# A hybrid decoder layer on one core: the transposed half of a triangular inverse made by transposing, and decode's value products moved to GpSimd

## The chip, the cores and the metric

The program runs on one core of one Trainium2 chip. Its time is the device time of one execution in microseconds; before the change the median of 3 runs was 1231.72 us (1231.1 to 1231.84). The profile shows one further execution.

## What is computed

One layer of a hybrid decoder is applied to a prompt of 512 tokens and to a sample group of 8 sequences with one token each. RMSNorm is followed by one input projection (2048 to 8208 columns), in which two mixers have their parts. All of it is fp32.

- Mixer A: softmax attention of 8 heads of 128 under three windows, (128,1), (512,4) and (2048,16), with RoPE on 32 dimensions. For a sample token, the keys and values of its 2048 cached positions are gathered: 128 keys for each of the three windows, and the token's own key in each of them. `o = softmax(q k^T / sqrt(128)) v`, merged over the windows by denominators, which is one softmax over 384 + 3 x 1 keys.
- Mixer B: gated DeltaNet, 8 heads of 128: causal convolution of width 4 and SiLU on q, k, v, then a delta rule in chunks. It needs the inverse of a triangular matrix:

```
a_mat = where(strict, einsum('bhnid,bhnjd->bhnij', kbeta, kc) * decay, 0.0)
t_mat = triangular_solve(a_mat + eye, eye, left_side=True, lower=True)
u = t_mat @ (v * beta);   w = t_mat @ (kbeta * exp(gcum))
```

- Both outputs are gated by SiLU of their own columns, go through one output projection, a norm and the residual.

## The kernel before

**Projection.** A weight tile (128 columns, 16 blocks of 128 rows) is split into a high and a low part in fp32r: ScalarE rounds `w_raw` to `w_hi` (`hi`, line 1006), and `w_lo` is the difference, made by VectorE for quarters 0 and 2 (`lo`, 1384) and by GpSimd for quarters 1 and 3 (`lo`, 1966). The hidden state is split the same way. TensorE's `segment` (583) does a quarter of a tile for one half of the tokens. Segments of half 0 have 8 wide and narrow matmuls, those of half 1 have 12. The half 0 result stands in one PSUM bank as two sums, which VectorE's `half_out` (1409) adds and copies out in segment 4 of a tile; the next tile's half 0 waits for that (`proj_half`).

**Steps.** A head has 8 tiles, 8 segments each: 64 steps, numbered 0 to 63. On every engine the same loop `stretch` runs: in each step it takes each of a list of generators one `yield` further, in the list's order, and after that the engine's own part of the projection is done (on VectorE `half_out` in segment 4, then `lo` in segments 0 and 4; on GpSimd `lo` in segments 2 and 6; on ScalarE `hi` in even segments; on SyncE the load of a weight quarter in even segments). `idle(n)` is n empty steps. So the order of each engine's instructions is written out by hand, and semaphores make an engine wait where another is behind. Work of head h-1's attention (`tail_a`, `attn_decode`) runs in head h's 64 steps, and after head 7 in a tail of 40 steps beside the output projection.

**Mixer B in the steps** (`mix_b`, lines 750, 1196, 1606, 2000; `own_b` makes the convolutions, `mix_q` q's part). A = kk^T times decay is made for four chunks of 128 tokens at once as a symmetrised matrix. The inverse is built by doubling the block size in levels n = 1 to 6. Two copies are kept: `b_U` holds the inverse of one orientation and `b_T` its transpose (chunks 0, 1 of U are one orientation and chunks 2, 3 the other, and the reverse in T). At each level: Y = B x T (line 801) into PSUM; ScalarE copies Y to `b_Y`; Z_U = Y^T x U (812) and Z_T = U^T x Y (820), blockwise; VectorE subtracts Z_U from U and Z_T from T (1658, 1659), and the next level begins. A level takes two steps; level 1 begins in step 36. B for each level is the masked A, made by GpSimd (2015).

**Decode of mixer A** (`attn_decode`, lines 430, 893, 1263, 1800). Scores are transposed (900), soft-maxed by 8 rows (1266 and 1803 to 1816), the probabilities transposed back with keys on partitions (906), and copied to `pT`. The values lie as keys x (sequence, dimension), one 128x1024 tile for each window, in `V_TILE`. ScalarE scales each 128x128 block by its column of pT (1281, 24 instructions), VectorE adds the three tiles (1819, 1822), and TensorE sums over the keys with eight products with a column of ones (911).

**RoPE** of q and k (`own_a`, 1515) is three instructions of VectorE on 32 rows (1511 to 1513).

Of the kernel before, what the change touches and what calls it, by code (L numbers as in the profile page):

```python
# [70 lines left out]
def layout(x):  # L71
# [8 lines left out]
    for name, order in (("cache_win_k", (0, 1, 2)), ("cache_win_v", V_ORDER)):  # L80
        c = x[name][0]
        windows = [c[:, PAST - 128:PAST], c[:, PAST - 512:PAST:4], c[:, 0:PAST:16]]
        t[name] = np.stack([windows[n] for n in order]).transpose(3, 0, 2, 1, 4)
# [91 lines left out]
def build(nc, x_prompt, x_sample, cache_k, cache_v, state_conv, state_delta, g_pre, w_in, w_ba, conv_w, a_log, dt_bias,  # L175
          onorm_w, w_out, g_post, c_ident, c_upper, c_causal, c_levels, c_lnmask, c_rope, c_terms,
          y_p, y_s, k_new, v_new, c_new, c_old, st_p, st_s):
    scratch_q = nc.dram_tensor("scratch_q", (NH, NB, HD), F32, kind="Internal").ap()
    scratch_g = nc.dram_tensor("scratch_g", (KT, P, TP), F32, kind="Internal").ap()

    with ExitStack() as ctx:
# [100 lines left out]
        pT = sb("pT", [P, 4, NB])  # L282
# [11 lines left out]
        xs_res = (S0[0:NB].rearrange("p b e -> p (b e)"), qb[0:NB])  # L294
        K_TILE, V_TILE = (kv[:, 0], kv[:, 1], kv[:, 0]), (kv[:, 1], kv[:, 0], qb[:])
# [25 lines left out]

        def mx(n):
            return MX[:, n].rearrange("p (c d) -> p c d", c=NC)
# [17 lines left out]
            "mix_kk mix_qk mix_A mix_QK mix_B mix_U0 mix_T_ps mix_T mix_Y_ps mix_Y mix_Z mix_UT ch_kS ch_r "  # L341
            "ch_v_ps ch_v ch_S_ps ch_o_ps ch_S ch_o1 ch_o o_sq on_rs o_n o_T z_sig_b z_ok_b gated_b gB_out S_out "

            "qkp qb_in kb0_in kb1_in kb2_in prod red sc_T sc_max p_exp p_norm p_T pT_ok vb0_in "
            "vb1_in vb2_in pv_sum pv_ps gated_ad "
# [22 lines left out]
        def _(sp):  # L368
# [61 lines left out]
            def attn_decode(hh, at=10):  # L430
# [3 lines left out]
                for n in (1, 2):  # L434
                    sp.dma_start(V_TILE[n].rearrange("p (b d) -> p b d", b=NB), cache_v[hh, V_SLOT[n]]).then_inc(
                        s[f"vb{n}_in"], 16)

            def attn_rows(h):
# [14 lines left out]
                if not first:  # L453
                    sp.wait_ge(s["pv_ps"], h)
# [54 lines left out]
            def early_rows():  # L509
                yield from idle(30)  # L510
                sp.wait_ge(s["gB_out"], 16 * (NH - 1))
                sp.wait_ge(s["gA_out"], 16 * (NH - 1))
                for k in (4, 5, 9):
                    load_row(k)
                yield from idle(25)
# [22 lines left out]
            work = [late_rows(), attn_decode(h, 6)]  # L538
# [43 lines left out]
        def _(pe):  # L582
# [167 lines left out]
            def mix_b(h):  # L750
# [3 lines left out]
                yield from idle(24)  # L754
                pe.wait_ge(s["kv_silu"], 2 * h + 2)
# [7 lines left out]
                for c in chunks:  # L763
                    last = pe.transpose(mx(1)[:, c, :], xv[:, c * P:(c + 1) * P], ident[:])
                last.then_inc(s["mix_T1"], 1)
# [4 lines left out]
                yield from idle(3)  # L770
# [20 lines left out]
                yield from idle(2)  # L791
                for n in range(1, LEVELS):
# [13 lines left out]
                    if n == 1:  # L806
                        pe.wait_ge(s["mix_U0"], 3 * h + 3)
                        pe.wait_ge(s["mix_ss"], 2 * NC * h + 2 * NC)
                        pe.wait_ge(s["mix_QK"], h + 1)
                    if n < LEVELS - 1:  # L810
                        for j in range(2):
                            last = pe.matmul(crossed(mx(2), n, True, j), b_Y[:, j, :], crossed(b_U, n, True, j),  # L812
                                             start=True, stop=True)
                    else:
# [7 lines left out]
                    last.then_inc(s["mix_Z"], 1)  # L822
# [28 lines left out]
            def mix_q(h):  # L851
                yield from idle(35)
                pe.wait_ge(s["q_silu"], h + 1)
                pe.wait_ge(s["mix_kbT"], h + 1)
                for c in range(NC):
                    last = pe.transpose(mx(2)[:, c, :], cq[:, c * P:(c + 1) * P], ident[:])
                last.then_inc(s["mix_T1"], 1)
                pe.wait_ge(s["mix_arg"], h + 1)
                for c in range(NC):
                    last = pe.matmul(mx(3)[:, c, :], xk[:, c * P:(c + 1) * P], cq[:, c * P:(c + 1) * P], start=True,  # L860
# [32 lines left out]
            def attn_decode(hh, late=0, sums=12, norm=5):  # L893
                yield from idle(17 + late)
# [7 lines left out]
                yield from idle(norm)  # L902
# [1201 lines left out]
```

## Time and profile before

| | |
|---|---|
| timed runs, median of 3 | 1231.72 us |
| the profiled execution | 1230.87 us |
| its span, first to last instruction | 1229.0 us |
| TensorE (PE) busy | 1201.0 us, 98% |
| weight loads (PEld) busy | 1123.0 us, 91% |
| VectorE (DVE) busy | 793.9 us, 65% |
| ScalarE (ACT) busy | 518.4 us, 42% |
| GpSimd (POOL) busy | 303.5 us, 25% |
| mean granted TensorE clock | 0.996 |
| moved by DMA | 151.55 MB, mean 123 GB/s |

The span is the time from the first to the last instruction; the profiled execution's own time holds 1.9 us more. Busy times overlap between engines. Matmuls are pipelined, so the record of one (0.28 us) is longer than the distance to the next (0.12 us); what a piece of work takes from TensorE is read from starts, not from durations. An fp32 matmul leaves two records, a transpose or an fp32r matmul one.

### The profile page before, as it was taken

The page shows a single profiled execution, that of the slowest core. Times are in us where ns is not written, and L with a number is a line of the kernel's source. Part 1 is how long each engine was busy: PE and PEld are TensorE (multiplying, and loading weights), DVE is VectorE, ACT ScalarE, POOL GpSimd, SP SyncE. Part 2 cuts the span into 40 slices and gives each one's busy share as a digit, 9 for nine tenths or more (in the row PEclk, how much of TensorE's full clock was granted, in tenths as well). Part 3 has the DMA queues.
Part 4 walks back from the last instruction along what each step waited for, and adds up shares of the span by engine and source line. Part 5 has one row for each costly group of instructions (what it writes and reads, how often), then busy time and mean ns, then how long its engine had stood idle before and what let it go on. Part 6 is the DMA issues. An engine that isn't in the chain of part 4 may idle for free.

```text
span 1229.0 us, 25525 instructions
## 1 busy us (share of the span) xinstructions
PE 1201.0 (98%) x8793; PEld 1123.0 (91%) x8793; DVE 793.9 (65%) x1945; ACT 518.4 (42%) x1376; POOL 303.5 (25%) x275
## 2 busy tenths in 40 slices
PE   5999999999999999999999999999999999999997
PEld 4899999999999999999999999999999998999996
DVE  5576577657765776577657765676567658365544
ACT  6443334533453345334533453345334536532211
POOL 0114121412141224122412241124212322322211
PEclk8999999999999999999999999999999999999999
DMA  7332453245324531453245324432453266232253
GB/s 244 100 95 63 141 165 104 63 140 166 103 63 141 164 103 63 143 163 103 63 144 162 104 62 144 161 104 62 147 159 104 88 196 202 82 103 78 93 207 139
DMA packets 79645, 151.55 MB, mean 123 GB/s; under 512 B 12353, under 2 KB 22242, under 8 KB 77986
## 3 DMA queue, kind: packets, MB, share of 16 engines
q1 hardware_dynamic: 78254, 148.78, 38.9%
q10 hardware_dynamic: 1312, 1.59, 0.5%
q8 instruction: 64, 1.05, 0.3%
q14 instruction: 15, 0.12, 0.0%
HBM read 132.20 MB, written 17.27 MB: 122 GB/s over the span
## 4 chain that ended last, share of the span: by engine, by line
PE 82%; DVE 8%; ACT 4%; issue 3%; DMA 1%; SPq 0%; DVEq 0%; ACTq 0%
PE PJ L614 17%; PE PJ L610 11%; PE PJ L611 10%; PE PJ L612 10%; PE PJ L615 9%; PE MX L820 3%; PE MX L801 2%; DVE memx L1578 1%; PE PJ L933 1%; PE MX L812 1%; PE MX L744 1%; PE MX L724 1%; PE PJ L934 1%; PE PJ L935 1%; PE MD L872 1%
## 5 line engine op out<-in xcount | busy, mean ns | idle before, releaser
L1966 POOL TENSOR_TENSOR w_lo<-w_raw,w_hi 128x512 fp32r<-128x512 f32 x160 | 218.1, 1363 | 808.2 <-ACT w_hi L1006 808.2
L614 PE MATMUL PJ<-h,w_hi 128*128 128x512 f32 x1110 | 416.8, 412 | 0.0
L610 PE MATMUL PJ<-h,w_hi 128*128 128x264 f32 (+1 forms) x1216 | 354.8, 292 | 0.0
L611 PE MATMUL PJ<-h,w_hi 128*128 128x264 f32 (+1 forms) x1216 | 344.7, 284 | 0.0
L612 PE MATMUL PJ<-h,w_lo 128*128 128x264 f32 (+1 forms) x1216 | 344.6, 283 | 0.0
L615 PE MATMUL PJ<-h,w_lo 128*128 128x256 f32 x1110 | 310.7, 280 | 0.0
L614 PEld LDWEIGHTS PJ<-h,w_hi 128*128 128x128 f32 x1110 | 208.9, 188 | 43.3 <-DVE w_lo L1384 1.7
L1006 ACT ACTIVATE w_hi<-w_raw 128x512 fp32r<-128x512 f32 x320 | 196.6, 624 | 91.3 <-PE PJ L612 79.1
L611 PEld LDWEIGHTS PJ<-h,w_hi 128*128 128x128 f32 x1216 | 229.6, 189 | 2.3
L610 PEld LDWEIGHTS PJ<-h,w_hi 128*128 128x128 f32 x1216 | 229.4, 189 | 0.0
L612 PEld LDWEIGHTS PJ<-h,w_lo 128*128 128x128 f32 x1216 | 228.2, 188 | 0.0
L615 PEld LDWEIGHTS PJ<-h,w_lo 128*128 128x128 f32 x1110 | 209.4, 189 | 2.8 <-issue 1.7
L1384 DVE TENSOR_TENSOR w_lo<-w_raw,w_hi 128x512 fp32r<-128x512 f32 x160 | 120.1, 756 | 131.5 <-ACT w_hi L1006 125.9
L1022 ACT ACTIVATE memx<-memx 128x520 f32<-128x520 f32 x32 | 20.2, 633 | 107.0 <-DVE memx L1589 107.0
L1578 DVE SCALAR_TENSOR_TENSOR memx<-memx,cw 128x512 f32<-128x512 f32 x72 | 61.2, 850 | 1.7
L1788 DVE CUSTOM_DVE_ANT_0 kv<-kv,qb 128x128 f32<-128x128 f32 x192 | 54.9, 342 | 2.5 <-DMA qb<-scratch_q 2.5
L1223 ACT ACTIVATE mem<-MX 128x256 f32<-128x256 f32 x48 | 18.3, 381 | 87.9 <-PE MX L801 87.9
L1658 DVE TENSOR_TENSOR mem<-mem,MX 128x256 f32<-128x256 f32 (+1 forms) x48 | 19.1, 398 | 54.5 <-PE MX L820 54.5
L933 PE MATMUL PJ<-h,w_hi 128*128 128x256 f32 (+1 forms) x160 | 47.3, 296 | 1.0 <-DVE h L1845 1.0
L2015 POOL TENSOR_TENSOR mem<-mem,levels 128x256 f32<-128x256 f32 x48 | 39.2, 817 | 26.6 <-PE MX L801 15.7
L1415 DVE TENSOR_REDUCE memx<-PJ 128x256 f32<-128x512 f32 x63 | 43.0, 683 | 3.6 <-DVE memx L1589 1.6
L934 PE MATMUL PJ<-h,w_hi 128*128 128x256 f32 (+1 forms) x160 | 45.1, 282 | 0.0
(334 smaller groups left out, 1841.2 us busy)
## 6 DMA issues: line engine op xcount, KB each, us to landing
w_raw<-in_w_in SPq DMA_DIRECT2D x256, 256.0 KB, 2.7
w_raw<-in_w_out SPq DMA_DIRECT2D x64, 256.0 KB, 2.9
kv<-in_cache_win_k SPq DMA_DIRECT2D x24, 512.0 KB, 4.6
kv<-in_cache_win_v SPq DMA_DIRECT2D x16, 512.0 KB, 4.9
out<-memx SPq DMA_DIRECT2D x16, 260.0 KB, 3.8
mem<-in_x_prompt SPq DMA_DIRECT2D x4, 1024.0 KB, 10.0
S<-in_state_delta SPq DMA_DIRECT2D x8, 512.0 KB, 3.4
out<-S SPq DMA_DIRECT2D x8, 512.0 KB, 2.9
```

Of the source, the lines that this page charges most:

```text
L610: pe.matmul(ps, wh, h_hi[:, k, tok], start=k == 0, stop=False)
L611: pe.matmul(ps, wh, h_lo[:, k, tok], start=False, stop=False)
L612: last = pe.matmul(ps, wl, h_hi[:, k, tok], start=False, stop=end)
L614: pe.matmul(both, wh, h2[:, :, k, tok], start=k == 0, stop=False)
L615: last = pe.matmul(ps, wl, h_hi[:, k, tok], start=False, stop=False)
L933: pe.matmul(out, wh, h_hi[:, k, tok], start=start and i == 0, stop=False)
L934: pe.matmul(out, wh, h_lo[:, k, tok], start=False, stop=False)
L1006: act.activation(w_hi[:, par, 4 * q:4 * q + 4, :], w_raw[:, q, :, :], ACT.Copy).then_inc(s["w_hi_ok"], 1)
L1384: dve.tensor_tensor(w_lo[:, par, 4 * q:4 * q + 4, :], w_raw[:, q, :, :], w_hi[:, par, 4 * q:4 * q + 4, :].bitcast(F32), ALU.subtract).then ...
L1578: link(dve.scalar_tensor_tensor(acc[:, 0:TP], xq[:, i:i + TP], w[:, 24 + i:25 + i], acc[:, 0:TP], ALU.mult, ALU.add))
L1788: last = dve.tensor_tensor_reduce(out=x, in0=x, in1=qb[:, b * HD:(b + 1) * HD], scale=1.0, scalar=0.0, op0=ALU.mult, op1=ALU.add, accum_ou ...
L1966: pool.tensor_tensor(w_lo[:, par, 4 * q:4 * q + 4, :], w_raw[:, q, :, :], w_hi[:, par, 4 * q:4 * q + 4, :].bitcast(F32), ALU.subtract).the ...
```

## The change

Two edits are made together.

**Inverse.** Level n = 1 to 5 no longer computes Z_T by products. Z_U goes to PSUM in an order in which the pair of orientations stands side by side (`merged` in place of `crossed`), ScalarE copies it to `b_Y[:, 2:4]`, VectorE subtracts it from U there, and one step later TensorE transposes the two 128x128 blocks into MX bank 3, from which VectorE subtracts T's update. A level takes three steps instead of two, and level 1 begins in step 34. TensorE:

```
 if n < LEVELS - 1:
     for j in range(2):
-        last = pe.matmul(crossed(mx(2), n, True, j), b_Y[:, j, :], crossed(b_U, n, True, j), start=True, stop=True)
+        last = pe.matmul(merged(mx(2), n, True, j), b_Y[:, j, :], crossed(b_U, n, True, j), start=True, stop=True)
+    last.then_inc(s["mix_Z"], 1)
+    yield
+    pe.wait_ge(s["mix_Zs"], (LEVELS - 2) * h + n)
+    for j in range(2):
+        last = pe.transpose(mx(3)[:, j, :], b_Y[:, 2 + j, :], ident[:])
+    last.then_inc(s["mix_Z"], 1)
...
-    last.then_inc(s["mix_Z"], 1)
-    for c in chunks if n < LEVELS - 1 else (2, 3):
-        last = pe.matmul(blocks(mx(3)[:, c, :], n, c // 2), b_U[:, c, :],
-                         blocks(b_Y[:, c % 2, :], n, c // 2), start=True, stop=True)
```

ScalarE and VectorE:

```
+                    if n < LEVELS - 1:
+                        act.wait_ge(s["mix_Z"], UTS * h + 2 * n - 1)
+                        act.activation(b_Y[:, 2:4, :], mx(2)[:, 0:2, :], ACT.Copy).then_inc(s["mix_Zs"], 1)
+                        yield
...
-                        u, uz = crossed(b_U, n, True), crossed(mx(2), n, True)
-                        t, tz = crossed(b_T, n, False), crossed(mx(3), n, False)
+                        u, uz = crossed(b_U, n, True), merged(b_Y[:, 2:4, :], n, True)
+                        t, tz = crossed(b_T, n, False), merged(mx(3), n, False)
...
                     dve.tensor_tensor(u, u, uz, ALU.subtract).then_inc(s["mix_UT"], 1)
+                    if n < LEVELS - 1:
+                        yield
+                    dve.wait_ge(s["mix_Z"], UTS * h + 2 * n)
                     dve.tensor_tensor(t, t, tz, ALU.subtract).then_inc(s["mix_UT"], 1)
```

**Steps that move with it.** `mix_b` begins a step earlier on every engine (TensorE 24 to 23, ScalarE 24 to 23, VectorE 25 to 24, GpSimd 22 to 21). v's transposes go a step behind k's. The convolution of q in VectorE's `own_b` begins in step 27 instead of 28 (`idle((10, 2, 6)[j])` becomes `(10, 2, 5)`), RoPE of q in step 44 instead of 43, k's stays in step 51. `mix_q` uses MX bank 0 in place of banks 2 and 3, and its products come two steps behind its transposes (37 instead of 35), behind ScalarE's squares; b_QK is made in VectorE's step 37 instead of 36.

**Decode's values.** The host lays the values out as dimension x (sequence, key). The normalised probabilities (8 x 384) are written to DRAM and read back three times, each to all 128 partitions, into `P_TILE` (the place of `probs` and `probT`). GpSimd multiplies the three 128x1024 tiles, VectorE adds them and reduces over the keys; ScalarE's 24 scalings, pT, the three small transposes and the eight one-column products are gone. The decode begins four steps earlier (TensorE 17 to 13). GpSimd and SyncE:

```
+            def attn_decode(hh, at=23):
+                yield from idle(at)
+                for n in range(3):
+                    if n == 0:
+                        pool.wait_ge(s["vb0_in"], 16 * hh + 16)
+                        pool.wait_ge(s["pb_in"], 48 * hh + 48)
+                    elif n == 1:
+                        pool.wait_ge(s["vb_in"], 32 * hh + 32)
+                    pool.tensor_tensor(V_TILE[n], V_TILE[n], P_TILE[n], ALU.mult).then_inc(s["prod"], 1)
+                    yield
+                    yield
...
+                yield from idle(out)
+                sp.wait_ge(s["p_norm"], hh + 1)
+                sp.dma_start(scratch_p[hh].rearrange("n b t -> b n t"), pd).then_inc(s["p_out"], 16)
+                yield from idle(back)
+                sp.wait_ge(s["p_out"], 16 * hh + 16)
+                sp.wait_ge(s["attn_ps"], hh + 1)
+                for n in range(3):
+                    sp.dma_start(P_TILE[n], scratch_p[hh, n].rearrange("b t -> (b t)").partition_broadcast(P)).then_inc(
+                        s["pb_in"], 16)
+                    yield
```

with out=7 and back=2: the store in SyncE's step 17, the broadcasts in 19, 20 and 21. VectorE:

```
-            def attn_decode(hh, late=0, sums=(9, 1, 4)):
-                yield from idle(17 + late)
+            def attn_decode(hh, late=0, gap=31):
+                yield from idle(13 + late)
...
-                yield from idle(sums[0])
+                yield from idle(gap)
                 dve.wait_ge(s["prod"], 3 * hh + 2)
                 link(dve.tensor_tensor(V_TILE[0], V_TILE[0], V_TILE[1], ALU.add))
-                yield from idle(sums[1])
+                yield
                 dve.wait_ge(s["prod"], 3 * hh + 3)
                 dve.tensor_tensor(V_TILE[0], V_TILE[0], V_TILE[2], ALU.add).then_inc(s["pv_sum"], 1)
-                yield from idle(sums[2])
+                yield
+                dve.wait_ge(s["pv_sum"], hh + 1)
+                dve.tensor_reduce(pv[:], V_TILE[0].rearrange("p (b t) -> p b t", b=NB), AX.X, ALU.add).then_inc(
+                    s["pv_ok"], 1)
+                yield
```

The sums are in steps 47 and 48 instead of 42 and 46. In the tail after head 7, the products are in GpSimd's steps 22, 24 and 26 and the sums, the reduction and the gate in VectorE's 27 to 30. The loads of three gated rows into places that `P_TILE` shares wait for head 6's products.

## Rows read from the trace of the kernel before

**Rows 1.** Table by windows, one whole head; busy us of each engine, then clock, DMA.
```profile
core 0: us, PE busy (x) PEld busy (x) DVE busy (x) ACT busy (x) POOL busy (x), PEclk, DMA share, GB/s
526.00:648.70 122.70, 122.49 (x894) 114.32 (x893) 82.83 (x213) 54.28 (x152) 31.33 (x29) 1.00 0.39 119
```

**Rows 2.** Waits of TensorE: waiting line, releaser, us in total, times, longest.
```profile
PE MX L856 <- DVE memx L1698: 1.5, 7, 0.2
```

**Rows 3.** Instructions in order of time, one level of the inverse: start, duration, what.
```profile
593.57 0.61 PE L812 MATMUL MX<-mem 128*128 128x128 f32 x4
594.02 1.00 PE L820 MATMUL MX<-mem 128*128 128x64 f32 x8
594.83 0.37 PE L610 MATMUL PJ<-h,w_hi 128*128 128x264 f32 x1
595.03 0.28 PE L611 MATMUL PJ<-h,w_hi 128*128 128x264 f32 x1
...
596.36 0.60 PE L801 MATMUL MX<-mem 128*128 128x128 f32 x4
596.72 0.37 PE L610 MATMUL PJ<-h,w_hi 128*128 128x264 f32 x1
...
597.00 0.39 ACT L1223 ACTIVATE mem<-MX 128x256 f32<-128x256 f32 x1 [2.01 <-PE MX L801]
```

**Rows 4.** The same view, two transposes of A between two segments.
```profile
580.39 0.38 PE L784 MATMUL MX<-ident,mem 128*128 128x128 f32 x2
580.53 0.48 PE L614 MATMUL PJ<-h,w_hi 128*128 128x512 f32 x1
```

**Rows 5.** The same view, decode's one-column products and small transposes.
```profile
567.41 0.33 PE L906 MATMUL MD<-ident,rb 8*128 8x8 f32 x3
567.67 0.66 PE L761 MATMUL MX<-ident,memx 128*128 128x128 f32 x4
...
620.01 1.84 PE L911 MATMUL MD<-ones,kv 128*128 128x1 f32 x16
621.71 0.47 PE L837 MATMUL MX<-mem 128*128 128x128 f32 x2
```

**Rows 6.** Groups of GpSimd's instructions: count, busy us, mean ns, idle before.
```profile
L1966 POOL TENSOR_TENSOR w_lo<-w_raw,w_hi 128x512 fp32r<-128x512 f32 x160 | 218.1, 1363 | 808.2 <-ACT w_hi L1006 808.2
...
L2023 POOL TENSOR_TENSOR S<-S,dd 128x1024 f32<-128x1024 f32 x8 | 15.2, 1898 | 9.8 <-PE MD L872 9.8
```

**Rows 7.** In order of time, GpSimd and VectorE side by side.
```profile
563.06 1.30 POOL L1966 TENSOR_TENSOR w_lo<-w_raw,w_hi 128x512 fp32r<-128x512 f32 x1 [7.44 <-ACT w_hi L1006]
...
563.22 1.16 DVE L1815 TENSOR_SCALAR dg<-ident,ds 8x8 f32<-8x8 f32 x1
```

**Rows 8.** In order of time, VectorE and TensorE around steps 28 and 29.
```profile
576.58 0.69 DVE L1415 TENSOR_REDUCE memx<-PJ 128x256 f32<-128x512 f32 x1
576.60 1.05 PE L779 MATMUL MX<-mem,memx 128*128 128x128 f32 x8
...
577.79 0.68 DVE L1628 TENSOR_TENSOR mem<-MX,mem 128x512 f32<-128x512 f32 x1
578.39 1.53 DVE L1578 SCALAR_TENSOR_TENSOR memx<-memx,cw 128x512 f32<-128x512 f32 x2
579.95 0.23 DVE L1583 TENSOR_SCALAR memx<-cw 128x8 f32<-128x8 f32 x1
...
581.01 0.43 DVE L1589 TENSOR_SCALAR memx<-memx 128x520 f32<-128x520 f32 x1
```

**Rows 9.** DMA issues: count, KB each, median us from issue to landing.
```profile
qb<-scratch_q SPq DMA_DIRECT2D x8, 512.0 KB, 4.7
```

**Rows 10.** In order of time, RoPE's second pass in step 43.
```profile
611.28 0.69 DVE L1512 TENSOR_TENSOR memr<-memr 32x520 f32<-32x520 f32 x1
```

**Rows 11.** In order of time, the tail: a conversion, the last row's split, its use.
```profile
1054.88 1.88 POOL L1966 TENSOR_TENSOR w_lo<-w_raw,w_hi 128x512 fp32r<-128x512 f32 x1 [5.97 <-ACT w_hi L1006]
...
1066.86 0.69 DVE L1845 TENSOR_TENSOR h<-gA,h 128x512 fp32r<-128x512 f32 x1
...
1071.43 0.28 PE L933 MATMUL PJ<-h,w_hi 128*128 128x256 f32 x1
```

More of the change, by code:

```diff
@@ L2 @@
 from contextlib import ExitStack
+import itertools
 import numpy as np
@@ L82, in layout @@
         windows = [c[:, PAST - 128:PAST], c[:, PAST - 512:PAST:4], c[:, 0:PAST:16]]
-        t[name] = np.stack([windows[n] for n in order]).transpose(3, 0, 2, 1, 4)
+        rows = (3, 0, 2, 1, 4) if name == "cache_win_k" else (3, 0, 4, 1, 2)
+        t[name] = np.stack([windows[n] for n in order]).transpose(rows)
     return t
@@ L294, in build @@
         xs_res = (S0[0:NB].rearrange("p b e -> p (b e)"), qb[0:NB])
+        P_TILE = [mem[:, 10 * TP + n * WA:10 * TP + (n + 1) * WA] for n in range(3)]
         K_TILE, V_TILE = (kv[:, 0], kv[:, 1], kv[:, 0]), (kv[:, 1], kv[:, 0], qb[:])
@@ L536, in late_rows, with last_decode @@
                 sp.dma_start(st_p[0, 0, h], S).then_inc(s["S_out"], 16)
-            work = [late_rows(), attn_decode(h, 6)]
+            def last_decode():
+                rows = attn_decode(h, 6, 5, 6)
+                yield from itertools.islice(rows, 17)
+                sp.wait_ge(s["h_lo_ok"], H_READY + split_at(9))
+                yield from rows
+            work = [late_rows(), last_decode()]
             for n in range(40):
@@ L769, in mix_b @@
                 last.then_inc(s["mix_gb"], 1)
-                yield from idle(3)
+                yield
+                pe.wait_ge(s["kv_silu"], 2 * h + 2)
+                for c in chunks:
+                    last = pe.transpose(mx(1)[:, c, :], xv[:, c * P:(c + 1) * P], ident[:])
+                last.then_inc(s["mix_T1"], 1)
+                yield from idle(2)
                 pe.wait_ge(s["mix_tok"], 3 * h + 1)
@@ L901, in attn_decode @@
                 last.then_inc(s["sc_T"], 1)
-                yield from idle(norm)
+                yield from idle(7)
                 pe.wait_ge(s["p_norm"], hh + 1)
-                pe.matmul(MD[:, 0, 3 * NB:4 * NB], ones[0:NB, :], dg[:], start=True, stop=True)
-                for n in range(3):
-                    last = pe.transpose(MD[:, 0, n * NB:(n + 1) * NB], pd[:, n, :], ident[0:NB, 0:NB])
-                last.then_inc(s["p_T"], 1)
-                yield from idle(sums)
-                pe.wait_ge(s["pv_sum"], hh + 1)
-                for b in range(NB):
-                    last = pe.matmul(MD[:, 0, 64 + b:65 + b], V_TILE[0][:, b * HD:(b + 1) * HD], ones[:, 0:1],
-                                     start=True, stop=True)
-                last.then_inc(s["pv_ps"], 1)
+                pe.matmul(MD[:, 0, 0:NB], ones[0:NB, :], dg[:], start=True, stop=True).then_inc(s["p_new"], 1)
             pe.wait_ge(s["memset_ok"], 1)
@@ L936, in unit @@
                 return last
-            work = [later(tail_a(NH - 1)), attn_decode(NH - 1, late=-10)]
+            work = [later(tail_a(NH - 1)), attn_decode(NH - 1, late=-6)]
             for n in range(40):
@@ L1325, in _ @@
             g_hi_samples(0, KT - 1)
-            work = [later(tail_a(NH - 1)), attn_decode(NH - 1, late=-10)]
+            work = [later(tail_a(NH - 1)), attn_decode(NH - 1, late=-6)]
             for n in range(40):
@@ L1855, in _ @@
             g_lo_samples(0, KT - 1, 5)
-            work = [last_keys(NH - 1, 4), later(tail_a(NH - 1)), attn_decode(NH - 1, late=-10)]
+            work = [last_keys(NH - 1, 4), later(tail_a(NH - 1)), attn_decode(NH - 1, late=-6, gap=17)]
             for n in range(40):
@@ L2048, in _ @@
             with repeat(pool, 1, NH) as h:
-                stretch(h, [tail_a(h - 1), own_b(h), own_a(h), mix_b(h), delta_decode(h)])
-            work = [later(tail_a(NH - 1))]
+                stretch(h, [tail_a(h - 1), own_b(h), own_a(h), mix_b(h), delta_decode(h), attn_decode(h - 1)])
+            work = [later(tail_a(NH - 1)), attn_decode(NH - 1, 22)]
             for n in range(40):
```

134 lines of the change are left out of this document (64 added, 70 removed).

## The prediction

> **What bounds the kernel now.** I read the table by windows first, then TensorE's waits, and then the instructions in order of time around the two edits. In one whole head TensorE is busy 122.49 of 122.70 us at granted clock 1.00, while VectorE has 82.83, ScalarE 54.28 and GpSimd 31.33 [rows 1]. The only wait of TensorE's that recurs from head to head is worth 1.5 us in seven times [rows 2]. So inside the heads nothing but TensorE's own instructions sets the pace: an instruction taken from it is a gain, and a new wait of it is a loss. The other engines are hidden, each by a margin of one or two steps, and the change spends part of these margins.
>
> A step is one segment of 12 projection matmuls and the generators' work behind it. After work of another kind the first projection matmul takes 0.20 us to the next (594.83 to 595.03) where others take 0.12, so each insertion costs 0.08 beside its own length; a segment is 1.45 us by itself and 1.53 behind an insertion (594.83 to 596.36) [rows 3].
>
> **Inverse, what TensorE saves.** One level before: four records for the U half, then eight of 64 columns for the T half, 593.57 to 594.83, plus 0.08: 1.34 us. After: four records as in the Y product (596.36 to 596.72, 0.36, plus 0.08) and, one step later, two transposes (580.39 to 580.53, 0.14, plus 0.08): 0.66 [rows 3, 4]. That is 0.68 for each of 5 levels and 8 heads: 27.2 us. The sixth level stays.
>
> **Decode's values, what TensorE saves.** Sixteen one-column records leave (620.01 to 621.71, 1.70) and three small transposes (567.41 to 567.67, 0.26) [rows 5]: 1.96 for each of 8 heads, 15.7 us. ScalarE loses 24 scalings and one copy a head and gets five 128x256 copies; it was hidden, so that is worth nothing by itself. Against it stand three more insertions a head (v's transposes, the p_new product and q's products, now each alone in a step): 3 x 0.08 x 8 = 2 us. TensorE's sum: 27.2 + 15.7 - 2 = 40.9 us.
>
> **What GpSimd gets.** Three products of 128x1024 a head. A 128x512 difference takes it 1.27 undisturbed (the mean of all is 1.363), so 2.54 each; the 128x1024 scaling whose second operand is a broadcast took 1.90 [rows 6]. Ends 1.9 and 2.5; I take 2.5, since both operands are dense. GpSimd has room for 7.5 us a head. What counts is what it does to VectorE: an 8x8 scaling that began at 563.22 took 1.16 and ended with GpSimd's instruction (563.06 + 1.30) [rows 7]. [...]
>
> **Step 28, the first new wait.** The head's A chain and q's convolution come one step earlier. VectorE's step 28 is now, in this order: A = kk x D, which must wait for TensorE's kk product of step 28, two convolution passes, small ones and the clamp, and only then the reduction that empties the projection's first PSUM half. TensorE may not begin step 32 before that reduction. In the kernel before, the reduction (576.58) stood ahead of A (577.79) and had 3 us of room. Now, from the start of kk: product seen 1.15, A 0.60, two passes 1.56, small ones 1.06, clamp 0.35 (0.43 less its tail), reduction 0.69: 5.4 us [rows 8]. TensorE gets to step 32 in 0.81 (eight records, as from 594.02 on [rows 3]) + 1.53 + 1.45 + 0.14 + 1.53 = 5.5 us. The margin is nothing before GpSimd's products are counted. Those start when three broadcasts of 512 KB have landed (4.7 us each [rows 9]). The last two are issued at about step 23, behind a w_lo that VectorE makes late, so the products run over about steps 25 to 30, with a w_lo of 1.3 between them, beside the convolution. With the broadcasts so early that only the end of one product is left in step 28, 0.2 us is lost; with a product or a w_lo ahead of each pass, 4.4. I take the middle, 2.3, for 7 heads (head 0 has no decode beside it): 16.1 us. With products that are over before kk it would be nothing.
>
> **Step 44, the second.** RoPE of q moves from step 43 to 44. There VectorE now subtracts level 4's U half, does RoPE (three passes of 0.69, gaps and a transpose, 2.4 us), the reduction and w_lo (0.60 each, as from 577.79 to 578.39), and only in step 45 the T half, which TensorE needs for Y in step 46 [rows 8, 10]. From the start of Z: ScalarE's copy done at 1.03 (as 596.36 to 597.39 [rows 3]), U 0.4, then 2.4 + 1.2 + 0.4: 5.4. TensorE is there after 0.36 + 1.53 + 0.22 + 0.2 (d_outer) + 1.45 = 3.8. So 1.6 late, or 0.9 where w_lo comes behind T. I take 1.3 for 8 heads: 10.4 us. In the other levels T comes first in its step, ahead of reduction and w_lo.
>
> **The last head.** Its products feed a sum in step 28, a reduction in 29 and the gate in 30 of the tail. Before, the last h_lo row was begun at 1066.86 and TensorE used it at 1071.43, some 4 us later; after the gain that is 1069.5 [rows 11]. The third broadcast is behind GpSimd's w_lo of 1054.88 (1.88 long), so it lands near 1061.5; three products and two w_lo, 10.2, a sum and a reduction of some 1.2 each (an estimate, twice the 0.60 of 512 columns), 0.5 of small ones and 0.7 for the row end at 1075.3. Ends 0 and 5.8; I take 3, since the first two products need not wait long for each other.
>
> **Edits at nothing.** The values' new layout has as many packets; the sums and the reduction (1.2 us a head) lie beside the end of the inverse, in VectorE's spare third [rows 1]. SP now waits for p_norm and for its own store ahead of w_raw loads that are needed eight steps later; DMA has a share of 0.39 [rows 1] and takes 1.5 MB more a head. Without that cover each would cost its own length a head.
>
> **Sum.** 40.9 - 16.1 - 10.4 - 3 = 11.4 us. The profiled execution took 1230.87 (span 1229.0), which makes 1219.5; the median of the timed runs is 0.85 above it: 1220.3. Under 0.2% (2.5 us) is what I call no change.
>
> **Rivals.**
> A. No new wait: the products hold nothing that is late, and T of level 4 is on time. For it: TensorE has practically no wait today although some margins are as narrow (L856 waits 0.2 at its longest [rows 2]). Against: step 28 has no room even without products. 1231.7 - 40.9 = 1191.
> B. The forecast, with its own range 1208 to 1229.
> C. Slower: the products hold VectorE at each pass of step 28. At 4.4 us a head that is 31, with step 44 at 1.6 (13) and the tail at 5.8: 50 us against 40.9, 1241. It turns the sign where the wait at step 32 passes 3.9 us a head (27.5, beside 10.4 and 3). For it: the lock is complete in the row I read; against: GpSimd leaves gaps while it waits for w_hi, and the broadcasts may land earlier.
> D. Gain and waits cancel, 1229 to 1234: more wait than in B, less than in C.
> That TensorE's work does not shrink as said has nothing for it: the counts follow from the code.
>
> **Chances.** A 0.20, B 0.47, D 0.10, C 0.23. Faster is A and B, 0.67; within 0.2% is D, 0.10; slower is C, 0.23. The likeliest is B, 1220. The range goes from near A, 1197, to near C, 1239.
>
> **What would show it.** TensorE's instructions per head shrink by 5.1 us, and 64-column products remain at level 6 alone. Its waits name VectorE's reduction of the first half at step 32, 1 to 4 us a head, and the T subtraction ahead of Y, about 1.3. Convolution passes of 0.75 stretch to 1.5 to 3 where a product of about 2.5 us runs. If TensorE shows no waits, A holds; if the products take under 2 us or run beside other work than q's convolution, my first wait is wrong; if T of level 4 is on time, the second is.

## The result

The changed kernel takes 1261.82 us (median of 4 runs, 1260.49 to 1262.44) where the kernel before, on the same chip, takes 1231.41 (4 runs, 1229.38 to 1231.84): 1.0244 times as long, 95% interval 1.0231 to 1.0256. It is 30 us slower; the forecast was 1220, and its range ended at 1239.

The page of the changed kernel: busy time of each engine, and TensorE's busy share and granted clock in 40 slices of the span.

```profile
span 1260.3 us, 24790 instructions
PE 1179.7 (94%) x8401; PEld 1097.5 (87%) x8401; DVE 845.2 (67%) x1953; ACT 473.9 (38%) x1216; POOL 367.4 (29%) x299
...
PE   5999998999899989998999899989998999799997
...
PEclk8999999999999989998999999989998999899999
```

TensorE is busy 21.3 us less than the 1201.0 of before, as was wanted, but in a span that is 31.3 us longer. So its idle time has grown from 28.0 to 80.6 us. The dips in both lines come once a head. The view of the waits says what they are (line, releaser, us in total, times, longest):

```profile
PE PJ L642 <- DVE memx L1427: 34.3, 7, 5.5
PE MX L831 <- DVE mem L1677: 12.0, 8, 1.7
...
PE PJ L961 <- DVE h L1872: 7.1, 1, 7.1
...
PE MX L803 <- DVE mem L1632: 1.8, 8, 0.2
PE PJ L961 <- DVE h L1867: 1.5, 1, 1.5
```

L642 is the first projection matmul of step 32, L1427 the reduction of the first PSUM half; L831 is Y, L1677 the T subtraction; L961 is the output projection in the tail, L1872 splits the last gated row's part of the samples, and L1867 is here the split of four earlier rows at the tail's start. Before, the only such wait from head to head was 1.5 us in all [rows 2]. The first product of the kk group shows where in the kernel the time goes (last figures: first and last start, us); here before, then after.

```profile
L779 PE MATMUL MX<-mem,memx x64: 272/275/275, 86.9 to 945.4; 128*128 128x128 f32 x64
```

```profile
L809 PE MATMUL MX<-mem,memx x64: 272/275/275, 86.2 to 962.1; 128*128 128x128 f32 x64
```

16.7 us are lost by the kk of head 7, the other 14.6 behind it, in head 7's second half and the tail.

Now one head from kk on: first GpSimd, then VectorE, in order of time. These are the instructions of [rows 8] in the changed kernel.

```profile
582.69 5.16 POOL L2067 TENSOR_TENSOR kv<-kv,mem 128x1024 f32<-128x1024 f32 x2 [6.42 <-DMA mem<-scratch_p]
587.81 1.71 POOL L1988 TENSOR_TENSOR w_lo<-w_raw,w_hi 128x512 fp32r<-128x512 f32 x1
589.48 2.33 POOL L2067 TENSOR_TENSOR qb<-qb,mem 128x1024 f32<-128x1024 f32 x1
```

```profile
584.00 0.69 DVE L1640 TENSOR_TENSOR mem<-MX,mem 128x512 f32<-128x512 f32 x1 [2.19 <-PE MX L809]
584.61 3.79 DVE L1590 SCALAR_TENSOR_TENSOR memx<-memx,cw 128x512 f32<-128x512 f32 x2
588.43 1.12 DVE L1595 TENSOR_SCALAR memx<-cw 128x8 f32<-128x8 f32 x1
589.59 2.52 DVE L1598 SCALAR_TENSOR_TENSOR memx<-cw,memx 128x8 f32<-128x8 f32 x2
...
592.75 0.68 DVE L1427 TENSOR_REDUCE memx<-PJ 128x256 f32<-128x512 f32 x1
```

GpSimd works without a break from 582.69 to 591.81. A (L1640), which reads one operand from PSUM, takes 0.69 in the middle of a product. The two convolution passes behind it read SBUF twice and take 3.79 in place of 1.53, and then the small instructions on 8 columns wait too: 1.12 in place of 0.23, 2.52 in place of some 0.5. The reduction ends at 593.43, and TensorE, which was through at 588.50, begins step 32 at 593.58.

The table by windows shows the second loss (busy us of TensorE, count, then its clock):

```profile
584.00:588.50 4.50, 4.50 (x38) 4.28 (x36) 4.43 (x4) 0.00 (x0) 4.50 (x3) 1.00 0.07 21
588.50:593.58 5.08, 0.00 (x1) 0.03 (x1) 4.94 (x7) 0.64 (x1) 3.31 (x2) 0.69 0.19 52
593.58:597.10 3.52, 3.52 (x11) 3.06 (x12) 3.27 (x6) 2.60 (x6) 2.09 (x2) 0.50 0.35 86
597.10:604.00 6.90, 6.90 (x49) 6.39 (x48) 3.91 (x13) 2.55 (x12) 2.96 (x3) 0.99 0.27 76
```

Within the wait the granted clock falls to half (from 1.00 to 0.50), and the first 3.5 us of work behind it run at that level: 11 records in 3.5 us, where the next stretch has 49 in 6.9. A pair of projection matmuls (L642 and L643) takes 0.64 us there and 0.35 behind it (594.36 to 595.00, 597.66 to 598.01). The low level begins at 590.4, 1.9 us into the wait, and ends at 597.2. It came with each of the seven waits at step 32, in three heads for about 3.4 us and in four for about 6.8. The prediction had no term for this.

### The profile page after: what moved, and what is told of

It is laid out like the page before. It is cut to its first block and busy times, and to the rows that moved or that the text cites. A ratio compares the mean times of both kernels' runs of the same rounds, so it can differ in the third digit from the quotient of the medians.

```text
span 1260.3 us, 24790 instructions
## 1 busy us (share of the span) xinstructions
PE 1179.7 (94%) x8401; PEld 1097.5 (87%) x8401; DVE 845.2 (67%) x1953; ACT 473.9 (38%) x1216; POOL 367.4 (29%) x299
## 5 line engine op out<-in xcount | busy, mean ns | idle before, releaser
L642 PE MATMUL PJ<-h,w_hi 128*128 128x512 f32 x1110 | 429.1, 422 | 34.3 <-DVE memx L1427 34.3
L643 PE MATMUL PJ<-h,w_lo 128*128 128x256 f32 x1110 | 315.4, 284 | 0.0
L642 PEld LDWEIGHTS PJ<-h,w_hi 128*128 128x128 f32 x1110 | 214.2, 193 | 79.7 <-issue 35.6
L640 PEld LDWEIGHTS PJ<-h,w_lo 128*128 128x128 f32 x1216 | 228.3, 188 | 0.0
L643 PEld LDWEIGHTS PJ<-h,w_lo 128*128 128x128 f32 x1110 | 214.4, 193 | 2.8 <-issue 1.7
L1396 DVE TENSOR_TENSOR w_lo<-w_raw,w_hi 128x512 fp32r<-128x512 f32 x160 | 124.3, 782 | 69.7 <-ACT w_hi L1034 67.0
L1590 DVE SCALAR_TENSOR_TENSOR memx<-memx,cw 128x512 f32<-128x512 f32 x72 | 85.6, 1189 | 1.8
L1673 DVE TENSOR_TENSOR mem<-mem 128x256 f32<-128x256 f32 x40 | 22.8, 571 | 53.8 <-ACT mem L1253 52.8
L961 PE MATMUL PJ<-h,w_hi 128*128 128x256 f32 (+1 forms) x160 | 49.1, 307 | 8.6 <-DVE h L1872 7.1
L2067 POOL TENSOR_TENSOR kv<-kv,mem 128x1024 f32<-128x1024 f32 x16 | 40.0, 2521 | 50.7 <-DMA mem<-scratch_p 50.7
L1806 DVE CUSTOM_DVE_ANT_0 kv<-kv,qb 128x128 f32<-128x128 f32 x192 | 50.9, 320 | 1.8 <-DMA qb<-scratch_q 1.7
L1427 DVE TENSOR_REDUCE memx<-PJ 128x256 f32<-128x512 f32 x63 | 43.2, 686 | 12.3 <-DMA out<-memx 10.7
L962 PE MATMUL PJ<-h,w_hi 128*128 128x256 f32 (+1 forms) x160 | 47.1, 294 | 0.0
```

What stands on the lines that cost most here:

```text
L640: last = pe.matmul(ps, wl, h_hi[:, k, tok], start=False, stop=end)
L642: pe.matmul(both, wh, h2[:, :, k, tok], start=k == 0, stop=False)
L643: last = pe.matmul(ps, wl, h_hi[:, k, tok], start=False, stop=False)
L961: pe.matmul(out, wh, h_hi[:, k, tok], start=start and i == 0, stop=False)
L962: pe.matmul(out, wh, h_lo[:, k, tok], start=False, stop=False)
L1396: dve.tensor_tensor(w_lo[:, par, 4 * q:4 * q + 4, :], w_raw[:, q, :, :], w_hi[:, par, 4 * q:4 * q + 4, :].bitcast(F32), ALU.subtract).then ...
```

## The experiments

My theory after the two traces: (1) the 4.9 us a head at step 32 are GpSimd's long products, which hold VectorE's convolution passes and the small instructions behind them (the lock theory); (2) each such wait costs some 2 us of clock beside itself (the clock theory). The rival to (1) was that the moved order alone has no room in step 28 (the order theory); to (2), that the slow matmuls came from something else than the wait. Each run is compared with runs of the kernel before on the same chip.

**The inverse edit alone (e1).** Decode's values stay as before (V_TILE by keys, ScalarE's scalings); all moved steps of mixer B are those of the change.

> The inverse edit with its moved steps, decode's values as before. Two theories of the 4.9 us a head by which VectorE's reduction was late for step 32. Lock theory: GpSimd's products hold q's convolution passes. Then this kernel has no wait at step 32 (under 0.3 us a head) and a granted clock of 1.00 in the heads; Y's wait for T at level 4 stays at 1.5 us a head, as nothing of GpSimd's is in it. Time: 1231.4 - 27.2 (inverse) + 1.3 (two insertions) + 12.0 + 1.8 = 1219 us. Rival, the order theory: the reduction now stands behind A and two passes, and that has no room by itself. Then most of the wait and of the lost clock stay: 34.3 and 12 us more, about 1250 to 1265 us.

Measured: 1227.45 us, ratio 0.9969 (0.9959 to 0.9978).

```profile
PE MX L810 <- DVE mem L1683: 12.0, 8, 1.7
...
PE MX L798 <- DVE mem L1653: 5.1, 7, 0.7
```

No wait at step 32: the reduction stands behind A and the passes here too, and is on time. The order theory falls. T of level 4 is late by the same 12.0 us as in the changed kernel, so this wait is the inverse edit's own. 8.5 us are missing against the expectation: 5.1 are a wait I had not seen (L798, the transposes of B0, for the level 0 mask on VectorE), and TensorE's busy time fell by 23.2 (1201.0 to 1177.8) where 25.9 were expected.

**The decode edit alone (e2).** The inverse and every step around it are those of the kernel before.

> Decode's values by dimension with products on GpSimd, the inverse and all steps around it as in the kernel before. Lock theory: the passes of q's convolution are stretched here too (one by 2 to 4 us), but the reduction stands ahead of them in step 28, so step 32 is not late; what comes behind the passes, A and the first products of the inverse, is late by 1 to 4 us a head. The tail loses about 8.6 us of waiting and 2.7 of clock. Time: 1231.4 - 15.7 + 0.6 + 11.3 = 1227.6 plus 7 to 28 us: 1235 to 1256 us. Order theory: the wait came from the moved steps alone, so only the tail costs: 1228 us.

Measured: 1262.18 us, ratio 1.0243 (1.0222 to 1.0265), just above the expected range. Its waits, then GpSimd and VectorE beside q's convolution:

```profile
PE MX L810 <- DVE mem L1629: 19.3, 7, 3.2
...
PE PJ L945 <- DVE h L1848: 7.8, 1, 7.8
...
PE MX L805 <- DVE mem L1622: 3.6, 6, 1.3
```

```profile
592.76 2.85 POOL L2043 TENSOR_TENSOR qb<-qb,mem 128x1024 f32<-128x1024 f32 x1
```

```profile
592.19 3.97 DVE L1572 SCALAR_TENSOR_TENSOR memx<-memx,cw 128x512 f32<-128x512 f32 x2
```

The edit that was to bring 15 us costs 30 by itself, as much as both edits together. In this order the reduction is ahead of the passes, so the lock comes out one link later, at the transposes of B0, with which the inverse begins: 2.8 us a head in the mean, 2.0 to 3.2. Behind it the granted clock is at 0.50 again in five heads of the seven (in this one from 599.4 to 602.8), which the expectation had left out: the waits of 3.2 us and of 2.94 lost it, of two of 2.95 one did and one did not, and so with two of 2.0.

**Tiny products (e3).**

```
-pool.tensor_tensor(V_TILE[n], V_TILE[n], P_TILE[n], ALU.mult)
+pool.tensor_tensor(V_TILE[n][:, 0:8], V_TILE[n][:, 0:8], P_TILE[n][:, 0:8], ALU.mult)
```

> The changed kernel with GpSimd's products cut from 1024 to 8 columns (the values are left unweighted in the rest); every wait, broadcast and step stays. Lock theory: the wait at step 32 is gone (under 0.3 us a head), the clock stays at 1.00 in the heads, the tail's wait shrinks to under 2 us; T of level 4 is as late as before (12.0 us). Time: 1261.8 - 34.3 - 12.3 (clock of seven heads) - 8.6 - 2.7 = 1204 us. Order theory: the wait at step 32 stays near 4 us a head; only the tail's is gone: about 1250 us.

Measured: 1214.35 us, ratio 0.9856 (0.9838 to 0.9875). The same instructions of VectorE as above, from A to the reduction, in this kernel:

```profile
566.96 0.69 DVE L1640 TENSOR_TENSOR mem<-MX,mem 128x512 f32<-128x512 f32 x1 [2.20 <-PE MX L809]
567.57 1.53 DVE L1590 SCALAR_TENSOR_TENSOR memx<-memx,cw 128x512 f32<-128x512 f32 x2
569.13 0.23 DVE L1595 TENSOR_SCALAR memx<-cw 128x8 f32<-128x8 f32 x1
569.40 0.49 DVE L1598 SCALAR_TENSOR_TENSOR memx<-cw,memx 128x8 f32<-128x8 f32 x2
...
570.53 0.68 DVE L1427 TENSOR_REDUCE memx<-PJ 128x256 f32<-128x512 f32 x1
```

From A's start to the reduction's end 4.25 us, against 9.43 with the products: 5.2 us of lock a head. With the products gone, the wait at step 32 is gone and the clock stays full in the heads; in the tail, behind a wait of 1.8 us, it is at half from 1053.7 to 1057.1. The 10 us over the 1204 expected are again the wait for the level 0 mask (5.1 us), which the longer wait had covered, 3.3 us of waiting left in the tail, and a clock loss in the changed kernel of 13.2 us (below) where I had taken off 15.0.

**The reduction first (e4).** VectorE's `half_out` of step 28 is issued ahead of that step's generators.

```
+if seg == 4 and j == 3:
+    half_out(h, j)
 step(work)
-if seg == 4 and not (isinstance(h, int) and h == 0 and j == 0):
+if seg == 4 and j != 3 and not (isinstance(h, int) and h == 0 and j == 0):
     half_out(h, j)
```

> The changed kernel with VectorE's reduction of step 28 put ahead of that step's other work (A and q's convolution). Lock theory: TensorE no longer waits for the reduction, but the first updates of the inverse, which stand behind the locked passes on VectorE (A + A^T at 593.95, the level 0 mask at 594.39), are as late as they were; the wait moves to the transposes of B0 in the same step, 4 to 6 us a head, with the same loss of clock: 1252 to 1266 us. Order theory: the wait is gone, with its clock: 1261.8 - 46.6 = 1215 us.

Measured: 1260.80 us, ratio 1.0236 (1.0217 to 1.0254).

```profile
PE MX L819 <- DVE mem L1649: 31.3, 7, 4.9
PE MX L831 <- DVE mem L1679: 12.1, 8, 1.7
```

The wait at step 32 has only changed its name, from the reduction to the mask of level 0 (L1649). Whichever instruction is put ahead, what stands behind the lock on VectorE is late. Taking the named releaser out of the way gains nothing where a chain of several is held.

**The products on VectorE (e5).** One product of 128x1024 each in steps 34, 36 and 45, where its rows with tiny products show it idle; in the tail in three steps running. The load of row 9, the only one of the three gated rows whose place `P_TILE` really shares, is moved behind them.

```
+for n in range(3):
+    yield from idle(gaps[n])          # (18, 2, 9)
...
+    dve.tensor_tensor(V_TILE[n], V_TILE[n], P_TILE[n], ALU.mult).then_inc(s["prod"], 1)
```

> The changed kernel with the three products moved from GpSimd to VectorE, each into a place where its own row shows it idle after the broadcasts are in (steps 34, 36 and 45; in the tail steps 21 to 23). One product should take VectorE 1.22 us, as its sum of the same size does. Lock theory: with GpSimd's long instructions gone, no wait at step 32 for the reduction and no clock loss in the heads, as with tiny products: the waits left are T of level 4 (12 us), the transposes of B0 (5 us) and the row end in the tail (under 3 us): 1214 us, within 3. Rival: VectorE has no room for 3.7 us more a head, so new waits of 1 us or more a head come up, in the inverse above all: 1222 us or more.

Measured: 1219.77 us, ratio 0.9909 (0.9888 to 0.9931).

```profile
PE MX L832 <- DVE mem L1678: 12.1, 8, 1.7
...
PE MX L820 <- DVE mem L1648: 5.1, 7, 0.7
PE PJ L962 <- DVE h L1881: 4.3, 1, 4.3
```

The same two waits a head as with tiny products, and no new one of weight: the products cost TensorE nothing inside the heads. The time is 5 us over the tiny products and outside the 3 us that I had allowed. About half of that is the tail's wait (4.3 for 1.8), where three products and two sums now stand on one engine ahead of the last row; I had forecast under 3 there. Behind it the clock is at half for 6.8 us, where behind the 1.8 it was for 3.4. The rest I have not split.

**All three: products on VectorE, the reduction first, RoPE of q back in step 43 (e6).**

```
-                yield from idle(44)
+                yield from idle(43)
                 rope_on(xa, s["q_swap"], 32 * h + 32, s["q_ok"])
...
-                yield from idle(7)
+                yield from idle(8)
```

> As e5, with two more steps put right: VectorE's reduction goes ahead of the other work of step 28, and RoPE of q goes back from step 44 to 43. If the two waits of TensorE that e1 and e3 still show come from the places of these two (T of level 4 behind RoPE, 12.0 us; the level 0 mask behind the reduction and so beside a w_lo of GpSimd's, 5.1 us), both go and the time is 1214 - 17 = 1197 us. Rival: RoPE in step 43 holds the U half of level 4 instead, or A comes later behind the reduction, so that one wait only changes its name: 1202 to 1214 us.

Measured: 1195.32 us (1194.99 to 1197.27), ratio 0.9708 (0.9688 to 0.9728).

```profile
PE PJ L962 <- DVE h L1883: 3.0, 1, 3.0
```

Both waits of the heads are gone and nothing took their place. T of level 4 kept its 12.1 us with the reduction first alone, so its end is RoPE's; which of the two steps freed the mask of level 0 was not tried alone. This kernel is 36 us faster than the one before and 66 faster than the changed one, with all of the change's arithmetic.

**The inverse edit alone, with the same two steps put right (e7).**

> The inverse edit alone (as e1) with the same two steps put right. If the two waits go: 1227.5 - 17.1 = 1210 us. If one only changes its name: 1215 to 1222 us. Its distance to e6 is what the decode edit is worth once its products lock nothing: 15.7 - 0.6 = 15 us less the tail, forecast 13.

Measured: 1219.54 us, ratio 0.9897 (0.9872 to 0.9922): the second case. VectorE in step 43, and the wait:

```profile
598.01 1.21 DVE L1845 TENSOR_TENSOR kv<-kv 128x1024 f32<-128x1024 f32 x1
599.36 1.32 DVE L1531 TENSOR_TENSOR memx<-memx,memr 32x520 f32<-32x520 f32 x1
600.71 1.05 DVE L1532 TENSOR_TENSOR memr<-memr 32x520 f32<-32x520 f32 x1
...
602.75 0.66 DVE L1797 TENSOR_TENSOR S<-S,MD 128x512 f32<-128x512 f32 x1
```

```profile
PE MD L906 <- DVE S L1797: 8.9, 7, 1.3
```

T of level 4 is on time, but decode's first sum, which the old decode has in this stretch, and RoPE now both stand ahead of the state's addition, and TensorE waits for that. A step is a free place only for one list of neighbours. Against this kernel the one with all three is 24.2 us faster; 8.9 of them are this wait, so the decode edit is worth about the 15 us that were forecast for it once it locks nothing.

**Pauses in the kernel before (p1, p2, p3, p5).** ScalarE makes n copies of 128x384 into a spare tile once TensorE's segment of step 11 is over, and TensorE waits for the last.

```
+def pause(h):
+    yield from idle(11)
+    act.wait_ge(s["proj_ps"], 16 * h + 5)
+    for n in range(2):                 # 2, 4, 6 or 9
+        last = act.activation(idle_out[:], ones[:].unsqueeze(1).to_broadcast((P, 3, P)), ACT.Copy)
```

Nine copies:

> The kernel before, with a pause of TensorE made in step 11 of heads 1 to 7: it waits until ScalarE has made nine copies of 128x384, begun when TensorE's segment of that step is over (about 5 us). Nothing else is added. Clock theory: a wait of this length brings the granted clock to half for about 3.5 us after it, which costs 1.7 us beside the wait: 7 x (5 + 1.7) = 47, so 1279 us, and a granted clock of 0.5 is seen behind each pause. Rival (the half speed in the changed kernel came from something else than the wait, such as the work around it): 7 x 5 = 35, 1267 us, clock 1.00.

Two, four and six copies, expected with the result of nine at hand:

> The kernel before with a pause as in the run with nine copies (there 4.4 us of wait in each of seven heads and 48.6 us in all), now with two copies: a wait of about 0.9 us a head. Clock theory, with a bound between the 1.8 us that left the clock at 1.00 and the 3.2 us that did not: no loss of clock, 7 x 0.9 = 6 us, 1238 us. Rival (each wait costs speed in proportion): 0.55 of the wait on top, 1241 us.

> The same with four copies: a wait of about 1.9 us a head. Clock theory: clock 1.00, 7 x 1.9 = 13 us, 1245 us. Proportional rival: 1252 us.

> The same with six copies: a wait of about 2.9 us a head. It tells on which side of the bound 2.9 us lies: with the clock at 1.00, 7 x 2.9 = 20 us, 1252 us; with a half clock behind it, 2.5 us a head more as in the run with nine copies, 1269 us. Proportional rival: 1263 us.

| copies | wait a head, us | 7 waits in all | time, us | ratio (interval) | over the waits |
|---|---|---|---|---|---|
| 2 | 0.5 | 3.6 | 1237.59 | 1.0056 (1.0037 to 1.0075) | 2.4 |
| 4 | 1.6 | 11.4 | 1245.40 | 1.0106 (1.0084 to 1.0128) | 2.4 |
| 6 | 2.7 | 19.1 | 1256.67 | 1.0220 (1.0191 to 1.0249) | 5.9 |
| 9 | 4.4 | 30.8 | 1280.08 | 1.0398 (1.0374 to 1.0422) | 17.8 |

The clock in the 14 us from the start of the copies, in two heads that follow each other, with six copies; and with nine copies the stretch behind the wait, in the first head with one and in the next:

```profile
306.48:320.48 14.00, 11.27 (x74) 0.88 0.36 121
433.59:447.59 14.00, 11.27 (x81) 1.00 0.37 121
```

```profile
186.80:190.00 3.20, 3.20 (x17) 3.20 (x16) 1.40 (x2) 2.09 (x4) 1.00 (x1) 0.50 0.27 67
313.00:319.60 6.60, 4.76 (x21) 4.76 (x22) 2.52 (x4) 4.53 (x9) 1.27 (x1) 0.50 0.17 55
```

In the profiled executions the clock fell with nine copies in each of the seven heads (for about 3.4 us in the first, for about 6.8 in the six others, the end of the wait included), with six in exactly every second one (three, about 3.4 us each), with four in none. So the wait by itself, with everything else as before, brings the fall, and neither rival stands: it is no share of each wait. Six copies came out between the two times that I had named (1252 and 1269), since some heads fell and others did not; one of their four timed runs took 1262.34 us at a mean clock of 0.985 where the others had 0.993 or more, so the share of the heads seems not to be fixed.

No single length divides the waits. In the heads those up to 1.7 us, the ones at step 44 included, left the clock alone in every trace, and those from 3.1 us on all lost it; 2.7 us lost it in three cases of seven, 2.9 to 3.0 in two of three, 2.0 in one of two. But in the tails waits of 1.4 to 1.8 us, all for the split of gated rows, were followed by a fall in five cases of ten: in the kernel with four copies (1.44), in the changed kernel (1.53), in the kernel with all three edits (1.54), in the inverse edit with its two steps put right (1.53) and with tiny products (1.77). The bound from which I had started, that 1.8 us leave the clock at 1.00, does not hold there. What the tail has that the heads have not is open, and so is why a wait of one length, 2.7 us, falls in every second head.

**Short products (e8).** In the changed kernel GpSimd makes each product of 1024 columns as eight of 128.

> The changed kernel with each of GpSimd's products of 1024 columns made as eight of 128 columns. GpSimd's work stays in its place and grows a little. If VectorE waits for one instruction of GpSimd's only and gets in behind it, a pass waits some 0.4 us in place of up to 2.5: the wait at step 32 falls from 4.9 to under 2 us a head and the clock stays at 1.00: 1261.8 - 7 x 3 - 13 = 1228 us, within 6. Rival: GpSimd keeps the lock through a row of instructions, or the longer row takes as much as it gives: 1255 us or more.

Measured: 1270.97 us, ratio 1.0310 (1.0285 to 1.0335). A miss in the time, and both halves of it are in the rows. The group of GpSimd's products, VectorE's two passes beside them, and the waits:

```profile
L2069 POOL TENSOR_TENSOR kv<-kv,mem 128x128 f32<-128x128 f32 x128 | 65.6, 551 | 52.0 <-DMA mem<-scratch_p 52.0
```

```profile
589.14 1.85 DVE L1590 SCALAR_TENSOR_TENSOR memx<-memx,cw 128x512 f32<-128x512 f32 x2
```

```profile
PE MX L831 <- POOL mem L2037: 23.4, 7, 3.4
...
PE PJ L961 <- DVE h L1872: 9.9, 1, 9.9
PE PJ L642 <- DVE memx L1427: 6.7, 7, 1.1
PE PJ L642 <- POOL w_lo L1988: 5.5, 6, 1.6
```

The two passes take 1.85 us in place of 3.79, and the wait for the reduction falls from 34.3 to 6.7: VectorE does wait for one instruction of GpSimd's at a time here and gets in behind it, for GpSimd's row of sixteen such products runs from 587.03 to 595.31, and both passes end inside it, at 590.99. But a piece of an eighth of the columns took 0.55 us, and eight take 4.1 to 4.4 where one took 2.5. GpSimd is 5.0 us a head longer at it (100.3 us in all against 60.1), and its own later work, w_lo and the masks of the levels (L2037), is late for TensorE.

## Why the prediction was wrong

Its sum, against what the changed kernel's profile shows:

| term | forecast, us | measured, us |
|---|---|---|
| TensorE's work | -40.9 | -34.5 |
| step 28/32, the reduction | +16.1 | +34.3 |
| step 44/46, T of level 4 | +10.4 | +12.0 |
| tail | +3 | +7.6 |
| half clock behind long waits | not priced | +13.2 |
| other idle time | 0 | -1.3 |
| sum | -11.4 | +31.3 |

The saving is the fall of TensorE's busy time with tiny products (1201.0 to 1166.5), whose instructions on TensorE are the same and run at full clock in all heads; the changed kernel's own fall is 21.3, and the 13.2 between them is the cost of the half clock. These two lines are good to 1.5 us or so: the kernel with tiny products has one half clock of 3.4 us in its own tail, and the traces differ by as much at their starts. The tail is 7.1 + 1.5 less the 1.0 that it had before. The last line takes in L803's 1.8 and the small waits of before that are gone.

**TensorE's work.** The counts were right, the sizes too large by 16%. In one head of the kernel with tiny products the inserted pieces take 5.6 us less than before, but the projection matmuls between them, without the waits, some 1.2 more. A level costs 0.38 + 0.17 and two restarts of 0.08, 0.71 against the forecast 0.66, and the new places of single insertions break more segments than I counted. Some 2 of the 6.4 us missing are the level; I have not split the rest.

**Step 28, the failed step.** The place, the releaser and the instruction held were as forecast, and so was the margin: from kk's start to the reduction's end I had 5.4 us without products, and the kernel with tiny products took 5.4, which is just on time. What failed is the size of the lock, "with a product or a w_lo ahead of each pass, 4.4. I take the middle, 2.3". The measured wait was 4.9 a head, above the upper end. Two reasons. The products did not run over steps 25 to 30 but started with kk (582.84): three broadcasts take 5.5 us each at the median, not 4.7 [rows 9]; the last two are issued at 575.2 to 576.1, in step 23 as forecast, but the products can begin only at 582.7, 6.6 us behind the last issue, and all 9 us of GpSimd's row lie on step 28's chain. And I counted only the two passes as held; VectorE's rows show two instructions of 8 columns held as well (0.9 and 2.0 us), each to the end of the GpSimd instruction that was running (589.52 and 591.81). One is a TENSOR_SCALAR, with a single tensor and a factor for each partition. So what counted here was how many instructions met one of GpSimd's, not their length: the two of 8 columns were held for 2.9 us together, the two passes of 512 for 2.3. Taking the middle of two ends was no reading of the rows: an issue in step 23 and 4.7 us to landing, both the prediction's own figures, put the products at about 580.7 to 590 on this trace, beside both passes, and that decided between the ends.

The product itself took 2.52 us (forecast 2.5; the group's row in the changed kernel):

```profile
L2067 POOL TENSOR_TENSOR kv<-kv,mem 128x1024 f32<-128x1024 f32 x16 | 40.0, 2521 | 50.7 <-DMA mem<-scratch_p 50.7
```

[rows 7] had shown the complete lock in one instance, an 8x8 scaling of 1.16 us; that passes of 512 columns are held as well was my estimate from it, and none of the prediction's rows shows it; the changed kernel's do (3.79 for two in place of 1.53). Rival C, which took the lock for the whole of step 28, had it right; at 0.23 I gave it half the chance of the middle. Its waits, 31, 13 and 5.8, add up to 50 us where 53.9 were measured; the rest of its distance is the clock and the smaller saving.

**Step 44.** 1.5 us a head, forecast 1.3, between the ends. RoPE in step 43 removes it, as the kernel with all three shows. This step had been moved for no gain that I could see, and moving it back was worth 12 us of waiting.

**The tail.** The wait for the last row is 7.1 us, over the upper end of 5.8; the other 1.5 is for rows at the tail's start, and the inverse edit alone has it too. The first product starts at 1083.7, when all three broadcasts have landed, and a w_lo of GpSimd's stands behind it, while VectorE's first sum takes 3.41 in place of 1.22 beside a product and a w_lo:

```profile
1090.18 3.41 DVE L1837 TENSOR_TENSOR kv<-kv 128x1024 f32<-128x1024 f32 x1 [3.54 <-POOL kv L2067]
```

**The clock, the missing term.** The prediction priced a wait at its length. In the head that I read, TensorE has no pause and a clock of 1.00 [rows 1]. But the same trace had the price at its start, where I had not looked. Its first matmuls wait, and then the table by windows shows half the clock:

```profile
18.38 3.65 PE L645 MATMUL MX<-ident,mem 128*128 128x128 f32 x16 [4.13 <-DVE h L1445]
```

```profile
17.80:24.20 6.40, 5.82 (x28) 5.38 (x29) 5.00 (x8) 3.93 (x5) 0.00 (x0) 0.50 1.02 197
```

Not every kernel's trace has this at its start, but a forecast of waits of 2 to 4 us in a kernel that else never paused should have carried it, as an open end of the range. With it even the forecast's own Rival C, 1241, comes to about 1254. The waits of step 44, 1.7 us at the longest, cost no clock: the kernels that have only these in their heads kept 1.00 there.

**The chances.** Without any lock the sum would have been right in sign and 13 us off in size: 1214 with tiny products, against 1231.7 - 40.9 + 10.4 = 1201 by the forecast's terms, and 5.1 of the distance is a wait that I had not seen, behind a w_lo of GpSimd's that holds the level 0 mask (1.49 in place of 0.42).

## What to carry to other kernels

Before long instructions are moved to GpSimd, list VectorE's instructions that will run beside them (those held here read SBUF alone; A, with one operand in PSUM, kept its 0.69 us), work out from the transfers when that will be, and charge each one that meets a GpSimd instruction with that instruction's rest, however small it is (here 0.9 and 2.0 us on instructions of 8 columns); a product of 1.22 us on VectorE in a stretch where its row shows it idle may be worth more than one of 2.52 us on an idle engine beside it. Where TensorE never pauses, price a new wait with the half clock that can follow it: in the heads here it came behind each wait of 3.1 us or more and behind some of 2.0 to 3.0, at 1.5 to 2.5 us each. Look for such a stretch in the trace at hand, at its start and end too. And ask for each new wait what is late next: twice here the wait only changed its name. Test the edits of a double change alone: one of the two was worth 4.6 us as it stood, the other cost 30.

## What the runs showed of the hardware

- TensorE's granted clock fell to half (0.50) in the heads with waits of 4.4 us in seven of seven, of 2.7 us in three of seven, alternately, and of 1.6 us in none; in the tails it fell behind five of ten waits of 1.4 to 1.8 us. In the heads it stayed at half for about 3.4 or about 6.8 us, in the tails up to 10.2 behind a wait of 7.1 (the changed kernel) and 13.7 behind one of 9.9 (short products), and a fall could begin before the wait was over (590.4, where the wait was 588.5 to 593.6). With nine copies the time over the waits was 17.8 us for seven, some 2.2 us each when the small overhead of the shorter pauses is taken off; with six, a head with the fall took 127.1 us and one without it 125.6.
- Beside GpSimd's products, A (PSUM and SBUF) took 0.69 us on VectorE, as it does without them (0.69 with tiny products); the instructions behind it, which read SBUF alone, were held, passes of 512 columns (3.79 us for two, 1.53 unheld) and instructions of 8 columns (1.12 for 0.23, 2.52 for 0.49) alike.
- GpSimd's 128x128 product took 0.55 to 0.58 us, the 128x1024 one 2.52 and the 128x8 one 0.23 to 0.26 (means of their groups): cutting work on it into eight instructions cost 1.7 us for each 1024 columns. VectorE's 128x1024 product took 1.22.
